# Two decoder blocks on one core: the first block's output projections in three fp32r passes, low parts moved to VectorE, the last squares of each norm summed on TensorE, conversions in a new order

## What is computed

```python
for layer in (0, 1):                      # first block
    hn = rms_norm(h, norm_g[layer])
    h = h + (even_layer if layer == 0 else odd_layer)(hn, ...)
# even_layer: q,k,v,gate_a,u,gate_b = hn @ w_in
#   att = windowed attention * silu(gate_a); ssm = s5 scan * silu(gate_b)
#   return concatenate([att, ssm]) @ w_out            # "ev_out"
# odd_layer: q,k,v,gate,qi,ki,wi = hn @ w_in; attention on the top 64 keys
#   return (att * silu(gate)) @ w_out                 # "od_out"
for i in (0, 1):                          # second block, x and a context of 256 tokens
    x, ctx = x + g1 * mixer(modulate(x)), ...         # 0: attention, 1: state space
    x = x + g2 * swiglu(modulate(x)); ...             # the modulations come from c @ ada_w
return rmsnorm(x, final_norm_g)
```

## Time and profile before

| | |
|---|---|
| time, median of 3 runs | 1574.89 us (1572.94 to 1576.03) |
| time of the profiled execution | 1572.72 us |
| its span, first to last instruction | 1570.6 us |
| mean granted TensorE clock | 0.972 |
| TensorE matmuls busy | 1480.5 us, 94% |
| VectorE / ScalarE / GpSimd busy | 751.3 / 613.6 / 279.0 us |
| read from and written to HBM | 202.76 MB and 2.62 MB |
| chain that ended last | TensorE 84%, VectorE 7%, DMA 3%, ScalarE 3% |

### The profile page before, as it was taken

How to read it: one execution, slowest core, us unless ns; L and a number is a source line. 1 busy time by engine, 2 the same in 40 slices (tenths; PEclk the granted TensorE clock), 3 DMA queues, 4 the chain that set the end, 5 groups by cost and what they waited for, 6 DMA issues and landing times.

```text
span 1570.6 us, 22847 instructions
## 1 busy us (share of the span) xinstructions
PE 1480.5 (94%) x9456; PEld 1251.9 (80%) x9456; DVE 751.3 (48%) x1225; ACT 613.6 (39%) x1151; POOL 279.0 (18%) x224
## 2 busy tenths in 40 slices
PE   7999999979998898999999998999999899999997
PEld 6878879857864586888888886778898678899997
DVE  6762144334449844323222333774453776455453
ACT  4424144233437725222122223452343474443342
POOL 2000177102000010211011111244500021021121
PEclk9799999899999999999999998999999999999998
DMA  7412464686200023313222233132351253645441
GB/s 233 161 32 104 137 249 158 225 364 253 108 28 1 28 101 141 131 59 120 106 96 84 93 113 119 58 108 81 126 194 57 82 188 141 236 172 202 174 166 39
DMA packets 36125, 206.84 MB, mean 132 GB/s; under 512 B 4968, under 2 KB 9496, under 8 KB 14904
## 3 DMA queue, kind: packets, MB, share of 16 engines
q1 hardware_dynamic: 32832, 199.58, 35.0%
q10 hardware_dynamic: 2376, 3.04, 1.0%
q0 software_dynamic: 816, 2.78, 0.5%
HBM read 202.76 MB, written 2.62 MB: 131 GB/s over the span
## 4 chain that ended last, share of the span: by engine, by line
PE 84%; DVE 7%; DMA 3%; ACT 3%; issue 1%; POOL 1%; SPq 1%; ACTq 0%; DVEq 0%; POOLq 0%
PE lin L1858 18%; PE lin L1860 17%; PE lin L1859 17%; PE lin L1825 4%; PE lin L1968 4%; PE modp L1896 2%; DMA ring<-ada_in 2%; PE lin L2484 1%; PE lin L1841 1%; PE lin L2433 1%; PE lin L1842 1%; PE lin L1843 1%; PE lin L2218 1%; PE aux L2360 1%; PE aux L1995 1%
## 5 line engine op out<-in xcount | busy, mean ns | idle before, releaser
L627 DVE TENSOR_TENSOR w_split<-ring,w_split 128x1024 fp32r<-128x1024 f32 (+1 forms) x140 | 187.8, 1347 | 347.1 <-ACT w_split L622 346.7
L622 ACT ACTIVATE w_split<-ring 128x1024 fp32r<-128x1024 f32 (+1 forms) x140 | 157.8, 1132 | 403.4 <-PE lin L1860 364.5
L1858 PE MATMUL lin<-hn_hi,w_split 128*128 128x512 f32 (+1 forms) x768 | 266.0, 346 | 3.5 <-DVE w_split L627 3.5
L1860 PE MATMUL lin<-hn_hi,w_split 128*128 128x512 f32 (+1 forms) x768 | 264.8, 345 | 0.0
L1859 PE MATMUL lin<-hn_lo,w_split 128*128 128x512 f32 (+1 forms) x728 | 249.2, 342 | 0.0
L1858 PEld LDWEIGHTS lin<-hn_hi,w_split 128*128 128x128 f32 x768 | 146.3, 191 | 20.9 <-issue 4.1
L1860 PEld LDWEIGHTS lin<-hn_hi,w_split 128*128 128x128 f32 x768 | 146.3, 190 | 17.2
L1859 PEld LDWEIGHTS lin<-hn_lo,w_split 128*128 128x128 f32 x728 | 138.8, 191 | 16.0 <-issue 0.5
L1859 PE MATMUL lin<-hid_split,w_split 128*128 128x512 f32 (+1 forms) x392 | 133.8, 341 | 0.0
L576 POOL TENSOR_TENSOR hn<-hn 128x256 f32<-128x256 f32 (+1 forms) x42 | 45.4, 1080 | 474.4 <-ACT hn L717 474.0
L1858 PE MATMUL lin<-hid_split,w_split 128*128 128x512 f32 (+1 forms) x352 | 118.5, 337 | 2.4 <-POOL hid_split L591 2.4
(11 more groups left out here) (461 smaller groups left out, 3067.7 us busy)
## 6 DMA issues: line engine op xcount, KB each, us to landing
ring<-ada_in SPq DMA_DIRECT2D x48, 1024.0 KB, 4.9
ring<-ssm_in_in SPq DMA_DIRECT2D x24, 1024.0 KB, 4.8
ring<-od_in_in SPq DMA_DIRECT2D x12, 1024.0 KB, 5.2
ring<-ffn0a_in_in SPq DMA_DIRECT2D x11, 1024.0 KB, 4.8
ring<-ffn0b_in_in SPq DMA_DIRECT2D x11, 1024.0 KB, 4.8
ring<-ffn1a_in_in SPq DMA_DIRECT2D x11, 1024.0 KB, 6.5
ring<-ffn1b_in_in SPq DMA_DIRECT2D x11, 1024.0 KB, 4.8
ring<-ev_in_in SPq DMA_DIRECT2D x9, 1024.0 KB, 13.5
```

What stands on the lines that cost most here:

```text
L622: act.activation(parts[:, 0], w, ACT.Copy).then_inc(sig("w_high"), 1)
L627: dve.tensor_tensor(parts[:, 1], w, parts[:, 0].bitcast(F32), ALU.subtract).then_inc(sig("w_low"), 1)
L1858: mm(lin[0:m, tile % RING, 0:width], hi, x_hi, start=kt == 0, stop=False)
L1860: ins = mm(lin[0:m, tile % RING, 0:width], lo, x_hi, start=False, stop=kt == kts - 1)
```

## The change

- `ev_out` and `od_out` become split matrices in the chain of parts of `od_in` (the same four places). `STREAM` reads all four blocks of `od_out` before `qkv`.
- Even output: ScalarE makes the high parts of weights and of `cat` (into `od_hi`) around the sigmoids, VectorE the low parts of `cat` (into `od_lo`) and of weights 4 to 7, GpSimd of weights 0 to 3.
- Odd input: VectorE makes the low parts of the activations, between its own products; ScalarE makes the activations' high parts before any weight's.
- Odd output: two new tensors for the parts of `q1`; ScalarE makes high parts of weights 0 to 3 and of `q1` in turn, VectorE the low parts of `q1` between its products, GpSimd the low parts of weights 0 to 4, VectorE of 5 to 7. The `qkv` parts come later, among the last squares and additions.
- Norms: the sum over the slices covers slices 0 to 6 only; TensorE adds slice 7 with a second matmul per 128 columns. Norms 2, 3 and 5 have `ada(2)` before and `ada(2)` behind.

```diff
-    ("od_small", 1, KT * SMALL), ("od_in", 12, 2 * KT * P), ("ada", 20, 2 * KT * P), ("od_out", 2, 2 * KT * P),
-    ("qkv", 2, 2 * KT * P), ("od_out", 2, 2 * KT * P), ("ada", 4, 2 * KT * P), ("qkv", 4, 2 * KT * P), ("w_o", 4, 2 * KT * P),
+    ("od_small", 1, KT * SMALL), ("od_in", 12, 2 * KT * P), ("ada", 20, 2 * KT * P), ("od_out", 4, 2 * KT * P),
+    ("qkv", 2, 2 * KT * P), ("ada", 4, 2 * KT * P), ("qkv", 4, 2 * KT * P), ("w_o", 4, 2 * KT * P),
...
-    ("od_in", 24), ("qkv", 12), ("w_o", 8),
+    ("ev_out", 8), ("od_in", 24), ("od_out", 8), ("qkv", 12), ("w_o", 8),
...
+        _, q1_lo, _, q1_hi = places(
+            ("q1_start", [P, 4096], F32), ("q1_lo", [P, KT, L], F32R), ("q1_between", [P, 1024], F32),
+            ("q1_hi", [P, KT, L], F32R))
...
         def sum_squares(pool, own, k, width):
...
             total = hn[:, 0, 0:width]
-            for kt in range(1, KT):
+            for kt in range(1, KT - 1):
                 pool.wait_ge(sig("squares"), KT * k + kt + 1)
                 ins = nc.gpsimd.tensor_tensor(total, total, hn[:, kt, 0:width], ALU.add)
-                if kt < KT - 1:
+                if kt < KT - 2:
                     own.link(ins)
             ins.then_inc(sig("square_sums"), 1)
...
-            if name == "od_in":
-                return name, w_split_od, W_UNITS, 0
+            if name in ("ev_out", "od_in", "od_out"):
+                return "ev_out", w_split_od, W_UNITS, 0
...
             before = lin_of[name] + u - chain(name)[2]
+            if name == "od_in" and u < W_UNITS:
+                before = lin_of["ev_out"] + KT - W_UNITS + u
...
+            for m in range(W_UNITS):
+                weights_lo(pool, "ev_out", m)
             sum_squares(pool, own, 1, L)
-            for m in range(2):
+            for m in range(24):
                 weights_lo(pool, "od_in", m)
-            for kt in range(KT):
-                pool.wait_ge(sig("od_high"), kt + 1)
-                pool.tensor_tensor(od_lo[:, kt, :], hn[:, kt, 0:L], od_hi[:, kt, :].bitcast(F32), ALU.subtract)\
-                    .then_inc(sig("od_low"), 1)
-            for m in range(2, 24):
-                weights_lo(pool, "od_in", m)
+            for m in range(5):
+                weights_lo(pool, "od_out", m)
             sum_squares(pool, own, 2, 2 * L)
...
         def second_block_scalar(act, own):
             full(act, "aux", aux_of["out1"] + 7)
-            for u in range(W_UNITS):
-                weights_hi(act, "qkv", u)
             act.wait_ge(sig("ctx_in"), 16)
-            act_norm(act, 2, 2 * L, "od_out", (0, 0, 0), True, later=6)
+            def od_weights(kt):
+                if kt < W_UNITS:
+                    weights_hi(act, "od_out", kt + W_UNITS)
+                for m in {4: (0, 1), 5: (2,), 6: (3,)}.get(kt, ()):
+                    weights_hi(act, "qkv", m)
+            act_norm(act, 2, 2 * L, "od_out", (0, 0, 0), True, before=od_weights, later=6)
...
-        def normed(dve, k, width, a, shifted=False, split=None, meanwhile=None):
...
                 ins.then_inc(sig("scaled" if shifted else "hn_ready"), 1)
                 if split is not None and kt >= 2:
                     low(kt - 2)
+                if behind is not None and kt >= 2:
+                    behind(kt - 2)
             if split is not None:
                 low(KT - 2)
                 low(KT - 1)
+            if behind is not None:
+                behind(KT - 2)
+                behind(KT - 1)
...
+            def cat_high(n):
+                if n < 4:
+                    taken(act, "aux", aux_of["out0"] + n)
+                else:
+                    act.wait_ge(sig("cat_ready"), n - 3)
+                act.activation(od_hi[:, n, :], cat[:, n, :], ACT.Copy).then_inc(sig("cat_high"), 1)
+            weights_hi(act, "ev_out", 0)
+            weights_hi(act, "ev_out", 1)
+            cat_high(0)
+            cat_high(1)
             for n in range(4):
                 tile = lin_of["glu"] + 2 * n + 1
                 full(act, "lin", tile)
                 frees(act.activation(qa[:, n], lin[:, tile % RING, 0:L], ACT.Sigmoid, bias=glu_b[:, 4 + n:5 + n]),
...
-            act_norm(act, 1, L, "ev_out", later=0)
-            for m in range(2):
-                weights_hi(act, "od_in", m)
+                if n < 2:
+                    cat_high(2 + n)
+                    weights_hi(act, "ev_out", 2 + n)
+                else:
+                    cat_high(2 + n)
+            cat_high(6)
+            cat_high(7)
+            def ev_weights(kt):
+                if kt < W_UNITS:
+                    weights_hi(act, "ev_out", kt + W_UNITS)
+            act_norm(act, 1, L, "ev_out", before=ev_weights, later=0)
             for kt in range(KT):
                 act.wait_ge(sig("hn_ready"), KT + kt + 1)
                 act.activation(od_hi[:, kt, :], hn[:, kt, 0:L], ACT.Copy).then_inc(sig("od_high"), 1)
-            for m in range(2, W_UNITS):
+            for m in range(W_UNITS):
                 weights_hi(act, "od_in", m)
...
+            weights_hi(act, "od_out", 0)
+            weights_hi(act, "od_out", 1)
+            for n in range(OD_HEADS):
+                taken(act, "aux", aux_of["out1"] + n)
+                act.activation(q1_hi[:, n, :], q1[:, n, :], ACT.Copy).then_inc(sig("q1_high"), 1)
+                if n % 4 == 3:
+                    weights_hi(act, "od_out", 2 + n // 4)
             second_block_scalar(act, own)
...
-            for kt in range(1, KT):
+            for kt in range(1, KT - 1):
                 dve.wait_ge(sig("squares"), kt + 1)
                 ins = tt(total, total, hn[:, kt, 0:L], ALU.add)
-                if kt < KT - 1:
+                if kt < KT - 2:
                     own.link(ins)
             ins.then_inc(sig("square_sums"), 1)
...
+            def cat_low(n):
+                dve.wait_ge(sig("cat_high"), n + 1)
+                tt(od_lo[:, n, :], cat[:, n, :], od_hi[:, n, :].bitcast(F32), ALU.subtract).then_inc(sig("cat_low"), 1)
...
                 tt(cat[:, 4 + n, :], qa[:, n], gate_b[:, n], ALU.mult).then_inc(sig("cat_ready"), 1)
+                cat_low(n)
+            for n in range(4, KT):
+                cat_low(n)
...
-            add_to_x("ev_out")
-            normed(dve, 1, L, lambda kt, s: gcol[:, 1, kt:kt + 1])
+            def ev_weights_low(n):
+                if n == 0:
+                    dve.wait_ge(sig("w_low"), unit_of["ev_out"] + W_UNITS)
+                if 0 < n <= W_UNITS:
+                    weights_lo(dve, "ev_out", n + W_UNITS - 1)
+            add_to_x("ev_out", ev_weights_low)
+            def od_low(kt):
+                dve.wait_ge(sig("od_high"), kt + 1)
+                tt(od_lo[:, kt, :], hn[:, kt, 0:L], od_hi[:, kt, :].bitcast(F32), ALU.subtract).then_inc(sig("od_low"), 1)
+            normed(dve, 1, L, lambda kt, s: gcol[:, 1, kt:kt + 1], behind=od_low)
...
+            def q1_low(n):
+                dve.wait_ge(sig("q1_high"), n + 1)
+                tt(q1_lo[:, n, :], q1[:, n, :], q1_hi[:, n, :].bitcast(F32), ALU.subtract).then_inc(sig("q1_low"), 1)
             for n in range(8):
                 tile = aux_of["out1"] + n
                 full(dve, "aux", tile)
                 frees(tt(q1[:, n, :], aux[:, tile % AUX, 0:L], gate1[:, n, :], ALU.mult), "aux", tile)
+                if n:
+                    q1_low(n - 1)
+            q1_low(KT - 1)
             modulations(dve, own, 0, 6)
             def query_weights(n):
-                if n % 2 == 0 and n < 4:
-                    for u in (n, n + 1):
-                        weights_lo(dve, "qkv", u)
+                if n == 2:
+                    dve.wait_ge(sig("w_low"), unit_of["od_out"] + 5)
+                for name, u in {2: (("od_out", 5),), 3: (("od_out", 6),), 4: (("od_out", 7),), 5: (("qkv", 0), ("qkv", 1)),
+                                6: (("qkv", 2),), 7: (("qkv", 3),)}.get(n, ()):
+                    weights_lo(dve, name, u)
             add_to_x("od_out", query_weights)
...
                 pe.wait_ge(sig("square_sums"), k + 1)
+                pe.wait_ge(sig("squares"), KT * (k + 1))
                 for n in range(width // P):
-                    ins = mm(aux[:, tile % AUX, n:n + 1], hn[:, 0, n * P:(n + 1) * P], ones[:, 0:1], start=True, stop=True)
+                    for kt in (0, KT - 1):
+                        ins = mm(aux[:, tile % AUX, n:n + 1], hn[:, kt, n * P:(n + 1) * P], ones[:, 0:1],
+                                 start=kt == 0, stop=kt > 0)
...
             for h in range(2):
                 taken(pe, "aux", aux_of["s5_y"] + h)
             linear("glu", "glu", 4, 4, lambda kt: u[:, kt, :])
-            pe.wait_ge(sig("cat_ready"), 4)
-            linear("ev_out", "ev_out", 2, KT, lambda kt: cat[:, kt, :])
+            split_linear("ev_out", KT, lambda kt: (od_hi[:, kt, :], od_lo[:, kt, :]), L, waits=("cat_low", 0))
...
-            for n in range(AUX):
-                taken(pe, "aux", aux_of["out1"] + OD_HEADS - 1 - n)
```

(12 more changed lines are left out.)

## The result

The changed kernel takes **1562.30 us** (median of 7 runs, 1558.8 to 1567.2) against 1572.94 us (1569.07 to 1578.83) for the kernel before on the same chip: a ratio of **0.9937**, 95% interval 0.9920 to 0.9954. Two further comparisons gave 0.9932 and 0.9927. It is faster by 9.9 to 11.5 us (1 minus the ratio, times the median beside it); 1568.6 with a range of 1562.5 to 1573.0 was forecast. The sign and the mechanisms held, and the gain came out larger than the 6.3 us of the sum.

A forecast was written before the change was run, and what follows sets the result against it. TensorE, busy for 94% of the span, and its waits were taken as the bound. Terms -5.2 + 0.7 - 1.5 - 0.3 = -6.3 us took 1572.7 to 1566.4 us profiled, 1568.6 as median; range 1562.5 to 1573.

The forecast's parts named there:

- Even output: Even output projection: eight units of 2.88 us take 23.0 instead of 27.89 us, ending at 189.3 against 194.6: 5.3 us won.
- The road to the odd input: Even projection to odd input: modulation blocks already landed, products at 194.9 instead of 202.38; 8.0 us together at full clock.
- The clock: At the first odd input the clock falls to half once, for 6.8 us: 2.8 us lost, bounds 0 and 5.1.
- Rival 1: No fall of the clock at the first odd input: -9.1 us, 1565.8 us; chance 17%.
- The first step together: Even output projection through the start of the odd input, loss by the clock included: 5.2 us won.
- Odd output: Odd output projection: `q1` low parts wait for GpSimd's conversions; third norm's products at 386.3 instead of 385.58: 0.7 us lost.
- Rival 2: At the odd output the low parts of `q1` aren't held up: 5.0 us more won, -11.3 us, 1563.6 us; chance 14%.
- Rival 3: Further clock loss at the odd output or its norm: +3.4 us or less, up to 1.6 in the norm; 15%.
- rival 4: Slower through the granted clock, losing from 18.2 us of new half-clock work: +2.7 us, 1577.6 us; chance 8%.
- Norm 5: Sixth norm, counted from 0: no more wait for the block that came at 1357.29: 1.5 us won.
- Norm 6: Norm numbered 6 from 0: GpSimd's sum goes, twice the matmuls come, table load ends at 1561.7: 0.3 us won.
- Norm 3: Norm numbered 3 from 0: fourth modulation block lands at 600.9 as before and TensorE waits: 0, upper bound 2 us.

The follow-up runs named there:

- e3_ev_out_f32: Changed kernel with the even output projection back in float32 and its conversions gone; 1568.53 us, ratio 0.9983 to the kernel before.
- e4_fill: Changed kernel plus seven overwritten matmuls filling TensorE's idle time ahead of the odd input; 1562.75 us, ratio 0.9939 to the kernel before.
- d_after: The changed kernel again, unedited, in the last side-by-side comparison of four; 1562.19 us, ratio 0.9927 to the kernel before.
- e7_dve_fill: Changed kernel with VectorE making the odd output's first two weight low parts and seven matmuls filling TensorE's wait before the odd input; 1557.42 us, ratio 0.9895.
- e2_low_on_dve: Changed kernel with VectorE making the odd output's first two weight low parts, GpSimd starting after all `q1` low parts; 1558.42 us, ratio 0.9909.
- c_after: The changed kernel again, unedited, beside three variants on one chip; 1561.43 us, ratio 0.9932 to the kernel before.
- e5_norms_old: Changed kernel with the norms' sums, matmuls and modulation blocks as in the kernel before; 1565.45 us, ratio 0.9952 to the kernel before.

## Why the prediction was right, and where its sizes were off

Its signs came as named: the even projection ended 22.5 us behind the last `cat` slice and no weight part held TensorE up, the first odd pass came behind GpSimd's low part at a clock of 0.50, and the held-up low parts of `q1` end just behind GpSimd's conversions. The third norm's products, forecast for about 380.8, came at 379.1, 378.2 and 381.0; the sixth norm's came 2.2 us earlier behind its projection, not 1.9 (6.80 and 4.56 us behind the last pass). Term by term:

1. *Even output.* Forecast: 5.3 us. From the last `cat` slice (ready at 166.7 before, 166.0 after) the first modulation block starts 27.9 and 22.6 us later: 5.3 us. The weight parts never held TensorE up, as costed: its one wait in that stretch is the 0.9 us for the last low part of `cat`.
2. *The road to the odd input.* "These have landed by then" was right: `e3_ev_out_f32`, with the old projection, still waited for a load between its blocks and took 6.7 us from the first block to the first product (193.63 to 200.36). The changed kernel took 5.4 (188.63 to 194.01; forecast 5.6), the kernel before 7.7. The first pass came 8.8 us behind the first product, forecast 9.1: VectorE's pairs follow at 0.73 us (195.28 to 196.01), not at the 0.82 that I summed from two durations.
3. *The clock.* One fall, 6.8 us: as forecast. It costs 2.5 us (`e4_fill`), 2.8 forecast. Rival 1, no fall, is out. `d_after` had 3.4 us of it in the same place, so its length isn't fixed.
4. *The first step together*: 5.2 us forecast. From the last `cat` slice to the last slice of the odd input it is 122.1 us before and 116.1 after, 6.0 us; 0.5 of the difference is the earlier first pass, 0.3 the clock. Undone alone (`e3_ev_out_f32`), the even output costs 7.1 us in the medians. This term was sized too small by 0.8 to 1.9 us.
   Behind it lies a stretch that the forecast didn't cost at all, from the last slice of the odd input to the first `q1` product: 58.2 us before, and 56.6, 56.3 and 58.1 in the three profiles of the changed kernel, 58.6 in `e3_ev_out_f32`. Of the 7.1 us of `e3_ev_out_f32` 2.2 lie there. It mostly goes with the clock in the attention: of these five profiles the three with 58 us and more have a fall of 10.2 us there (from between 289 and 296), the two with 56 one of 6.8; but `e7_dve_fill` has 58.2 us with one of 6.8. Up to 1.9 us of the gain lie in this stretch, and whether the change or chance put them there is open.
5. *Odd output.* Forecast 0.7 us lost. The stretch is 38.6 us before, and 38.1 to 40.3, mean 39.4, in the seven profiles with this order and the new norms: 0.7 more. As in my walk, three low parts were held up, one by each of GpSimd's first three conversions, for 1.0, 1.8 and 2.0 us. The third began 0.26 us behind the start of a conversion and ended 0.28 us behind its end. The Trainium skill (SBUF — State Buffer, SBUF: two separate sides) calls it an exclusive lock for the whole instruction; the trace agrees. Rival 2, low parts not held up, is out. It was priced at 5.0 us; `e2_low_on_dve` takes the hold-ups away, though VectorE then spends 2.4 us on the two conversions itself, and has the first unit done 4.3 us earlier. Of these 3.0 are left in the whole, as the clock falls ahead of the third norm.
6. *Rival 3*, a further fall while the odd output waits, happened: 6.8 us from 345.1, and 3.4 us at the third norm (from 379.3). TensorE worked at half clock through most of the first, but the first unit needs VectorE's last low part anyway: the second unit starts 0.9 us behind the end of that part, and 0.5 in `c_after`, where the fall had ended. So it cost 0.4 us. (By the prediction's own terms the worst case of this rival, 1.3 us under the kernel before, is about 1573.6 by the median, not the 1572 that it gives.) The 18.2 us of new half-clock work of rival 4 didn't come together.
7. *Norm 5*: 1.5 forecast, 1.3 measured (14.28 us from the chain's last pass ahead of the norm to the first behind it before, 12.98 after). In `e4_fill`, where the load came late, it is gone: from TensorE's last pass to its first it is 8.7 us there, 7.4 in the changed kernel and 8.8 before. *Norm 6*: 0.3 forecast; from the last addition to the reciprocal 2.95 us before (1559.45 to 1562.40), 2.64 after: 0.3.
8. *Norm 3*: forecast 0, with 2 us as the bound "if a shorter wait moves the half clock". It moved: the last block took 1.93 us before and 1.07 after, and undoing the norms brought the half clock and 2.4 us back. The other two profiles of the changed kernel have a fall of 3.4 us there that ends ahead of the last block. From the last pass before the norm to the first behind it, it is 11.1 us before and in `e5_norms_old` 11.2, and 10.0, 10.3 and 10.5 in the changed kernel. I counted in that row only the wait for the load, and not that the projection behind it ran at half clock too. Against the one profile of before the gain doesn't show, though: from the third norm to norm 4 it has 588.6 us and the changed kernel 588.7, which was at half clock three times for 3.4 us elsewhere in that stretch (from 468, 533 and 622). The first two of these stand in all thirteen profiles of the changed kernel and its variants, the third in eleven, so they seem to come with the change; with one profile of before, that is not shown.

So the terms that the runs settle are 6.0 to 7.1 for the first step, less 0.7, plus 1.6 for norms 5 and 6, plus 0 to 2.4 for norm 3: 6.9 to 10.4 us. The profiles differ by 8.0, the medians by 9.9 to 11.5; the profiled execution of the changed kernel was 2.3 us above its median. The sizes that the forecast had wrong are its first term (5.2 us, measured 6.0 to 7.1), the 0 of norm 3 (0 to 2.4), and the stretch in front of the `q1` products that it left out (0 to 1.9). Some us of the measured gain have no sure place. From norm 4's first product to norm 6's it is 589.8 us before, 588.2, 586.2 and 587.7 in the changed kernel, and 588.0 in `e5_norms_old`, whose norms are those of before: single profiles scatter there by as much as the forecast's 1.8 us.

## What to carry to other kernels

Three fp32r passes are only worth their shorter matmuls where the low parts can be made off the path. Here the even output had a gate's time for it; the odd one had none, and there the same edit earned nothing until VectorE made the first weights' low parts itself. Before you give a conversion to GpSimd, look at which two-operand SBUF instructions VectorE has in that stretch. Cost an idle stretch of TensorE by the rows behind it as well as by its own length, and look for what a local gain meets later: a fall of the clock or a load can take it back, as they did here with 1.2 of 4.3 us at the odd output and with the fill.

## What the runs showed of the hardware

- From the odd input to the last norm the granted clock fell for stretches of 3.4, 6.8, 10.2 or 13.7 us, at places that differ between profiles of the same code: at the odd input 6.8 us in two of them and 3.4 in the third (79.3 and 78.2 us for its passes). One profile can be off by more than a microsecond for this alone.
- The changed kernel reached its second norm at 194.01, 194.35 and 195.65 us in three profiles, and seven kernels with the same code up to there at 191.3 to 192.9. A gain of a few us should be read against a near milestone, not against the start.
- Keeping the clock up by filling an idle stretch did what it should where it was put, and nothing that could be measured in the whole time (-0.2 us in the mean of four comparisons).
- A VectorE subtraction with two SBUF operands that meets a GpSimd subtraction of 2.4 us under way ended 0.3 us behind it; a VectorE product with one PSUM operand took its 0.42 us beside it (340.69 to 345.53 in the changed kernel, product at 343.25).
